# Two-layer hybrid backbone on one core: gate and up products of the feed-forward blocks recast as seven quarter products, with the way down in six groups

## The chip, the cores and the metric

The kernel runs on one core of a Trainium2 chip. The metric is the device time of one execution in microseconds (us). All arithmetic is float32. A large matrix product is made of three passes: each operand is split into a rounded part ("hi", the type that TensorE takes in one pass, fp32r in the rows) and the rest ("lo"), and hi*hi, hi*lo and lo*hi are added up in PSUM.

## The reference, cut to what matters

There are 512 latent tokens and 256 context tokens, width 1024, and two layers. Each layer has a first feed-forward block, a mixer (input projection, four kinds of heads, output projection), and a second feed-forward block:

```
h  += 0.5 * gate1 * (silu(m @ Wg) * (m @ Wu)) @ Wdown      m = rmsnorm(h) * gain * (1 + scale) + shift
u   = modulated rmsnorm(h) @ W_in ; h += gate2 * heads(u) @ W_out
h  += 0.5 * gate3 * (silu(m @ Wg) * (m @ Wu)) @ Wdown
```

Wg and Wu are 1024 x 2816, Wdown is 2816 x 1024. Shift, scale and gate come from a conditioning product ("mod") that the kernel works out in the shadow of other work. So there are four feed-forward blocks. Three of them have all 768 tokens (called wide below); in the last one context tokens are no longer needed, so that it has 512 (called narrow).

## The kernel before, in words

Activations lie transposed: 128 features on the partitions, tokens along the free axis. The residual `h` is 8 tiles of 128 x 768. A weight block is 128 output columns by 1024 rows, 512 KB, as 8 tiles of 128 x 128.

The function `ffn` (from L539) is one feed-forward block. It goes over 22 pairs of blocks (one of gate, one of up), in two halves of 11, and after each half takes that half's 11 results through the way down: 8 output tiles, each the sum over 11 blocks of 128. For each weight block SyncE (SP) loads `raw[s]` (L207), ScalarE rounds it to `w_hi[s]` (`split_hi`, L217), VectorE makes `w_lo[s] = raw - w_hi` (`split_lo`, L222), and TensorE runs `product` (L240). Gate uses slot 0 and up slot 1, so that while TensorE works on one slot the other one is refilled:

```python
for k in range(kt):
    for w, m in ((w_hi[s], mov_hi), (w_hi[s], mov_lo), (w_lo[s], mov_hi)):
        for a, b, o in spans:
            mm = pe.matmul(out[:, o:o + b - a], w[:, k, :], m[:, k, a:b], ...)
```

With 768 tokens and two shift columns, `spans` are 512 and 258 columns; with 512 tokens they are 258 and 258. So a pair is 96 matmuls: 2 blocks x 8 k x 3 passes x 2 spans. The moving operand `hn_hi`/`hn_lo` is h times gain, without the norm's 1/rms; that factor (`rstd`) is multiplied in when a product leaves PSUM (L647 for gate, L657 for up). For this reason the first product of a block can begin before the sum of squares is known: `sums_pe` (L479) runs behind the first gate product, and ScalarE makes `rstd` by Ln (L467) and Exp (L471) after that. After a gate product ScalarE does Tanh and Identity (L600, L602), VectorE the silu product (L652) and the gated product (L663), and `g_hi`/`g_lo` are made by ScalarE (L607) and VectorE (L668).

On the way down `add_residual` (L533) adds a finished tile to `h` from PSUM, ScalarE and VectorE make the next phase's `hn_hi` (L447) and `hn_lo` (L457) from it, and GpSimd (POOL) adds its square up (`square_residual`: L500, L503, L505). GpSimd has nothing else to do in a feed-forward block. The three wide blocks also work out 24 columns of mod each: VectorE takes two products of 128 x 1024 for each (L287).

The queues are in order: SP issues the loads in the order of use, each behind a wait for the buffer; each engine runs its list. Loops are hardware loops except at the edges. Each phase is a `Block`, at whose start all engines begin together.

Of the kernel before, what the change touches and what calls it, by code (L numbers as in the profile page):

```python
# [14 lines left out]
F32 = mybir.dt.float32  # L15
# [57 lines left out]
def build_trunk(nc, A):  # L73
    with ExitStack() as ctx:
# [35 lines left out]
        WS = NFH * P * 4  # L110
# [18 lines left out]
        gate, glu = out_sb  # L129
        tanh_g = tmp("tanh_g", [P, NT])  # L130
# [54 lines left out]
        gate_scaled, up_scaled = sem("gate_scaled", 1), sem("up_scaled", 1)  # L185
# [138 lines left out]
        def setup():  # L324
            n_setup = [0]
            with nc.Block() as block:
# [12 lines left out]
                def _(pool):  # L339
                    for x in lo_ready + block_done + evacuated + shifted + [gate_scaled, up_scaled] + mod_used:  # L340
                        pool.sem_inc(x.sem, 1)
# [196 lines left out]

        def ffn(l, which, nt, following, mod_plan=None, more=True, fresh=False, nxt=None):  # L539
            part = 0 if which == 0 else 6  # L540
            gain = "n1" if which == 0 else "n2"

            PER_HALF = NFH + KD // 2

            MODS = (NFH + 2, NFH)
            ml, mj0 = mod_plan or (0, 0)
            mod_from = (mj0, mj0 + MODS[0])

            with nc.Block() as block:
                @block.sync  # L550
                def _(sp):
                    for half in range(2):
                        b0 = half * PER_HALF
                        j0 = mod_from[half]
                        def step(i, loads=True):
                            for s in range(2 if loads else 0):
                                load_block(sp, s, A["wgu"][l, which, i * 2 + (half * NF + s)], KD, i + b0)
                            if mod_plan:
                                mod_load(sp, ml, 0, i + j0, i + half * MODS[0])
                        if half == 0:  # L560
                            step(0, loads=False)
                        with sp.Fori(1 if half == 0 else 0, NFH) as i:
                            step(i)

                        def load_down(i):
                            for s in range(2):
                                load_block(sp, s, A["wdn"][l, which, half, i * 2 + s], NFH, i + (b0 + NFH))
                        load_down(0)
                        if mod_plan and half == 0:
                            for n in range(NFH, MODS[0]):  # L570
                                mod_load(sp, ml, 0, j0 + n, n)
                        with sp.Fori(1, KD // 2) as i:
                            load_down(i)
                    next_loads(sp, following, KD, 2 * PER_HALF)

                @block.gpsimd
                def _(pool):
                    if more:
                        square_residuals(pool, KD // 2)

                @block.scalar
                def _(act):
                    act.preload_act_table_set("natural_log_exp_and_others")
                    if fresh:
                        split_hi(act, 0, KD, 0)
                        shifts_hi(act, l, part, nt)
                        for k in range(KD - 1):
                            gained_hi(act, k, nt)
                    gained_hi(act, KD - 1, nt)
                    split_hi(act, 1, KD, 0)  # L590
                    rstd_act(act, nt, True)

                    def gate_up(i, half, last):
                        b0 = half * PER_HALF
                        nk = NFH if last else KD

                        split_hi(act, 0, nk, i + (b0 + 1))
                        act.wait_ge(gate_scaled.sem, i + gate_scaled.at(half * NFH + 1))
                        for span, w in tokens_of(nt):
                            act.activation(tanh_g[:, span], gate[:, span], ACT.Tanh, bias=gate[:, nt + w:nt + w + 1])  # L600
                        for span, w in tokens_of(nt):
                            mm = act.activation(gate[:, span], gate[:, span], ACT.Identity,  # L602
                                                bias=gate[:, nt + w:nt + w + 1])
                        mm.then_inc(tanh_ready.sem, 1)
                        split_hi(act, 1, nk, i + (b0 + 1))
                        act.wait_ge(glu_ready.sem, i + glu_ready.at(half * NFH + 1))
                        act.activation(g_hi[:, bass.ds(i, 1), 0:nt].rearrange("p a t -> p (a t)"), glu[:, 0:nt],  # L607
                                       ACT.Copy).then_inc(g_hi_ready.sem, 1)

                    def down(i, half, last):  # L610
                        for s in range(2):
                            if not last:
                                split_hi(act, s, NFH, i + (half * PER_HALF + NFH + 1))
                            elif half == 0:
                                split_hi(act, s, KD, PER_HALF)
                            elif s == 0 and following:
                                split_hi(act, 0, KD, 2 * PER_HALF)
                            if half == 1 and nxt and not (last and s == 1):
                                gained_hi_after(act, s, i * 2 + s, nxt[3], i + evacuated[s].at(KD // 2 + 1), nxt[4])
                    for half in range(2):  # L620
                        with act.Fori(0, NFH - 1) as i:
                            gate_up(i, half, False)
                        gate_up(NFH - 1, half, True)
                        if half == 1 and nxt:
                            shifts_hi(act, nxt[0], nxt[2], nxt[3], 1, nxt[4])
                        with act.Fori(0, KD // 2 - 1) as i:
                            down(i, half, False)
                        down(KD // 2 - 1, half, True)

                @block.vector  # L630
                def _(dve):
                    if fresh:
                        norm_gains(dve, l, gain, part)
                        shifts_lo(dve, l, part, nt)
                        split_lo(dve, 0, KD, 0)
                        for k in range(KD - 1):
                            gained_lo(dve, k, nt, hn_hi_ready.at(k + 2))
                    sums_dve(dve, nt, True)
                    gained_lo(dve, KD - 1, nt, hn_hi_ready.at(KD + 1))
                    split_lo(dve, 1, KD, 0)  # L640
                    dve.wait_ge(rstd_ready.sem, rstd_ready.at(1))

                    def gate_up(i, half, last):
                        b0 = half * PER_HALF
                        nk = NFH if last else KD
# [55 lines left out]
                def _(pe):  # L701
                    def gate_up(i, half, first=False, is_first=False):
# [6 lines left out]
                        if first:  # L709
                            sums_pe(pe, nt)  # L710
# [1897 lines left out]
```

## Time and profile before

| | |
|---|---|
| median of 3 runs | 3361.91 us (3359.94 to 3364.61) |
| profiled execution | 3367.02 us, span 3365.3 us |
| mean granted TensorE clock | 0.985 |
| PE busy | 3231.2 us, 96% of the span |
| VectorE (DVE) busy | 1817.0 us, 54% |
| ScalarE (ACT) busy | 1157.8 us, 34% |
| GpSimd (POOL) busy | 439.7 us, 13% |
| DMA | 263.34 MB, mean 78 GB/s |

PE is TensorE's matmuls and PEld its weight loads, which run beside them. "A x2" in a row of a timeline is two instructions merged; a duration of one matmul is longer than its distance to the next one, since they are pipelined, so that rates are read from how many there are in a stretch. Of the four feed-forward blocks the wide ones take from 46 to 610, 1278 to 1839 and 1841 to 2402 us of the span, the narrow one 2978 to 3356.

### The profile page before, as it was taken

What the parts mean: (1) busy time and instruction counts of PE and PEld (TensorE: products, weight loads), DVE (VectorE), ACT (ScalarE), POOL (GpSimd) and SP (SyncE); (2) the same over time, 40 slices, a digit from 0 to 9 for tenths busy, and PEclk for the clock granted to TensorE, in tenths of its full rate; (3) what the DMA queues carried; (4) which work ended last, traced back from release to release, by engine and by line L of the source; (5) the groups of instructions that cost most, each with busy time, mean ns of one, the idle gap of its engine ahead of it and who ended that gap; (6) DMA issues with size and microseconds to landing.
All of it is one profiled execution on the core that took longest, in us unless ns stands there. A gap on an engine that the chain in (4) does not pass through costs nothing. (4 is left out here: it accounts for less than half of the span.)

```text
span 3365.3 us, 67083 instructions
## 1 busy us (share of the span) xinstructions
PE 3231.2 (96%) x28066; PEld 2765.1 (82%) x28066; DVE 1817.0 (54%) x2677; ACT 1157.8 (34%) x1839; POOL 439.7 (13%) x312
## 2 busy tenths in 40 slices
PE   6999999999988999999999999999999989899998
PEld 5888888886667878888888888888886668789897
DVE  4552554565667655543554553454555766655353
ACT  3331222225665333321222431222224654344231
POOL 2000001000705310000002000001100616120000
PEclk9999999999999999999999999999999999999999
DMA  5231221342000012222221222222232000122222
GB/s 201 91 109 66 94 96 60 127 156 89 1 17 3 4 57 81 93 98 77 90 90 57 94 98 71 81 93 85 85 141 110 2 18 3 34 88 94 90 91 94
DMA packets 68270, 263.34 MB, mean 78 GB/s; under 512 B 7552, under 2 KB 8704, under 8 KB 67456
## 3 DMA queue, kind: packets, MB, share of 16 engines
q1 hardware_dynamic: 67664, 256.95, 22.1%
q10 hardware_dynamic: 432, 3.88, 0.3%
q8 instruction: 133, 2.18, 0.3%
q14 instruction: 41, 0.34, 0.0%
HBM read 258.70 MB, written 2.10 MB: 77 GB/s over the span
## 5 line engine op out<-in xcount | busy, mean ns | idle before, releaser
L240 PE MATMUL ps<-hn_hi,w_hi 128*128 128x512 f32 (+1 forms) x3520 | 864.8, 327 | 17.9 <-DVE hn_lo L457 5.9
L240 PE MATMUL ps<-hn_hi,w_lo 128*128 128x512 f32 (+1 forms) x3520 | 865.4, 327 | 0.0
L240 PE MATMUL ps<-hn_lo,w_hi 128*128 128x512 f32 (+1 forms) x3520 | 861.1, 326 | 0.0
L217 ACT ACTIVATE w_hi<-raw 128x1024 fp32r<-128x1024 f32 (+1 forms) x300 | 338.5, 1128 | 1375.4 <-PE ps L240 1217.7
L222 DVE TENSOR_TENSOR w_lo<-raw,w_hi 128x1024 fp32r<-128x1024 f32 (+1 forms) x300 | 396.9, 1323 | 469.5 <-ACT w_hi L217 462.0
L240 PEld LDWEIGHTS ps<-hn_hi,w_hi 128*128 128x128 f32 x3520 | 547.9, 190 | 82.3 <-issue 17.6
L240 PEld LDWEIGHTS ps<-hn_lo,w_hi 128*128 128x128 f32 x3520 | 548.3, 190 | 58.3
L240 PEld LDWEIGHTS ps<-hn_hi,w_lo 128*128 128x128 f32 x3520 | 545.2, 190 | 58.1
L240 PE MATMUL ps<-g_hi,w_hi 128*128 128x512 f32 (+1 forms) x1424 | 398.0, 347 | 6.1 <-DVE g_lo L894 6.1
L240 PE MATMUL ps<-g_lo,w_hi 128*128 128x512 f32 (+1 forms) x1424 | 403.5, 351 | 0.0
L240 PE MATMUL ps<-g_hi,w_lo 128*128 128x512 f32 (+1 forms) x1424 | 397.5, 347 | 0.0
L240 PEld LDWEIGHTS ps<-g_hi,w_lo 128*128 128x128 f32 x1424 | 228.5, 189 | 39.6
L240 PEld LDWEIGHTS ps<-g_hi,w_hi 128*128 128x128 f32 x1424 | 224.7, 188 | 43.7 <-DVE w_lo L222 6.9
L240 PEld LDWEIGHTS ps<-g_lo,w_hi 128*128 128x128 f32 x1424 | 226.7, 189 | 34.5
L500 POOL TENSOR_TENSOR out_sb<-h 128x768 f32<-128x768 f32 x5 | 7.3, 1469 | 1602.0 <-DVE h L533 1602.0
L647 DVE TENSOR_TENSOR out_sb<-ps,rstd 128x770 f32<-128x770 f32 (+1 forms) x88 | 78.6, 894 | 242.6 <-PE ps L240 215.7
L657 DVE TENSOR_TENSOR out_sb<-ps,rstd 128x770 f32<-128x770 f32 (+1 forms) x88 | 78.6, 894 | 183.7 <-PE ps L240 183.7
L607 ACT ACTIVATE g_hi<-out_sb 128x768 f32 (+3 forms) x88 | 69.9, 795 | 211.1 <-DVE out_sb L663 211.1
L668 DVE TENSOR_TENSOR g_lo<-out_sb,g_hi 128x768 f32 (+3 forms) x88 | 78.5, 892 | 93.4 <-ACT g_hi L607 93.4
L287 DVE SCALAR_TENSOR_TENSOR ps<-w_mod_one,cond_rows 128x1024 f32<-128x1024 f32 x100 | 122.8, 1228 | 10.7 <-DMA w_mod_one<-wmod 9.7
L287 DVE SCALAR_TENSOR_TENSOR w_mod_one<-w_mod_one,cond_rows 128x1024 f32<-128x1024 f32 x100 | 122.1, 1221 | 0.0
L457 DVE SCALAR_TENSOR_TENSOR hn_lo<-h,moda,hn_hi (+1 forms) x88 | 92.6, 1095 | 51.4 <-ACT hn_hi L447 51.3
(274 smaller groups left out, 3795.8 us busy)
## 6 DMA issues: line engine op xcount, KB each, us to landing
raw<-wgu SPq DMA_DIRECT2D x176, 512.0 KB, 3.4
w_mod_one<-wmod SPq DMA_DIRECT2D x100, 512.0 KB, 3.3
raw<-wdn SPq DMA_DIRECT2D x64, 704.0 KB, 4.1
raw<-win SPq DMA_DIRECT2D x44, 512.0 KB, 4.5
w_mod_two<-wmod SPq DMA_DIRECT2D x28, 512.0 KB, 3.6
w_mod_first<-wmod_first SPq DMA_DIRECT2D x4, 2048.0 KB, 23.2
raw<-wout SPq DMA_DIRECT2D x16, 512.0 KB, 3.3
h<-xT ACTq DMA_DIRECT2D x1, 3072.0 KB, 9.8
```

What stands on the lines that cost most here:

```text
L217: act.activation(w_hi[s][:, 0:kt, :].rearrange("p k n -> p (k n)"), raw[s][:, 0:kt * P], ACT.Copy).then_inc(hi_ready[s].sem, 1)
L222: dve.tensor_tensor(w_lo[s][:, 0:kt, :].rearrange("p k n -> p (k n)"), raw[s][:, 0:kt * P], w_hi[s][:, 0:kt, :].rearrange("p k n -> p (k n ...
L240: mm = pe.matmul(out[:, o:o + b - a], w[:, k, :], m[:, k, a:b], start=(k == 0 and w is w_hi[s] and m is mov_hi), stop=(k == kt - 1 and w i ...
L287: mm = dve.scalar_tensor_tensor(out=products if w else ps[:, 4:7:2, :], in0=products, scalar=1.0, in1=cond_rows[:, w, :].rearrange("p (a b ...
L457: mm = dve.scalar_tensor_tensor(out=hn_lo[:, bass.ds(tile, 1), to].rearrange("p a t -> p (a t)"), in0=h[:, bass.ds(tile, 1), span].rearran ...
L500: pool.tensor_tensor(sum_sq[:, 0:NT], hv, hv, ALU.mult).then_inc(sq_summed.sem, 1)
L607: act.activation(g_hi[:, bass.ds(i, 1), 0:nt].rearrange("p a t -> p (a t)"), glu[:, 0:nt], ACT.Copy).then_inc(g_hi_ready.sem, 1)
L647: dve.tensor_tensor(slot_like(gate, nt), slot_all(0, nt), slot_like(rstd, nt), ALU.mult).then_inc(gate_scaled.sem, 1)
L657: dve.tensor_tensor(slot_like(glu, nt), slot_all(1, nt), slot_like(rstd, nt), ALU.mult).then_inc(up_scaled.sem, 1)
L668: dve.tensor_tensor(g_lo[:, bass.ds(i, 1), 0:nt].rearrange("p a t -> p (a t)"), glu[:, 0:nt], g_hi[:, bass.ds(i, 1), 0:nt].rearrange("p a ...
```

## The change

In `ffn`, the gate block and the up block side by side are a matrix of 2 x 2 quarters: gate and up across, the first and the second 512 rows down. The moving operand is cut likewise: first and second 512 features, first and second half of the tokens. Before, their product is eight quarter products. The change forms them from seven, by the known scheme (Strassen's, in Winograd's form), with sums and differences of quarters on both sides.

- **TensorE**: a pair is 7 products x 4 k x 3 passes = 84 matmuls of 386 columns (258 in the narrow block), each product into one PSUM bank, eight banks in turn. The code is unrolled and has no hardware loops.
- **The moving side** is made once for each feed-forward block, at its start. `x_norm` is h times gain times `rstd` (so `rstd` has to be known before the first matmul), then come T1 to T4, differences and sums of its quarters, and hi and lo of all seven. VectorE, GpSimd and ScalarE share this. The sum of squares is moved in front of it all, with the last tile's squares on ScalarE.
- **The weight side** is made for every pair: four sums or differences of quarters (128 x 512), on GpSimd (on VectorE for the first pair), each written into the lo slot of its product as soon as that product of the pair before is done; then hi of the gate block (128 x 1024) and of five quarters by ScalarE, and lo of the gate block and of two quarters by VectorE, of three by GpSimd.
- **Out of PSUM**: ScalarE copies the first product, VectorE does seven additions of one bank each, and Tanh, silu, the gated product and the split are done in two halves of the tokens.
- **The way down** is in six groups of 4, 2, 4, 4, 4 and 4 pairs in place of two of 11. Of the first four output tiles all blocks but the group's last are taken first, then the last one of each; tiles 4 to 7 follow whole. `h` is added to 8 times in each group. While a group's down products run, the next pair's weights are made.
- Mod columns are still 24 in each wide block, 11 of them beside gate and up work and 13 on the way down. In `out_proj` (L864) and at the end of a feed-forward block that another follows, only the gained h is written (`gained_plain`), and the `hn_lo` work of VectorE goes. The host lays `wdn` out anew, with the same bytes.

The core of the diff:

```diff
-        WS = NFH * P * 4
+        WS = KD * P * 4 + 1568
...
+        SIZES = DOWN_SIZES
...
+            def weight_sum(eng, p, n):
+
+                a, b, op = {2: (quarter(2), quarter(3), ALU.add),
+                            3: (slot_sum[2][:, :], quarter(0), ALU.subtract),
+                            4: (quarter(0), quarter(2), ALU.subtract),
+                            5: (quarter(1), slot_sum[3][:, :], ALU.subtract)}[p]
+                if n:
+                    slot_free(eng, p, n)
...
+                eng.tensor_tensor(slot_sum[p][:, :], a, b, op).then_inc(w_summed.sem, 1)
...
+                    def up_raw_free(n):
+                        sp.wait_ge(w_summed.sem, w_summed.at(4 * n + 4))
+                        lo_there(sp, 6, n)
...
+                    pool.wait_ge(hn_hi_ready.sem, hn_hi_ready.at(KD + 1))
+                    for half in range(2):
+                        pool.wait_ge(rstd_ready.sem, rstd_ready.at(half + 1))
+                        pool.tensor_tensor(x_norm[:, half, LP:KD, 0:HT], gained_h[:, LP:KD, half * HT:(half + 1) * HT],
+                                           rstd_of(half), ALU.mult).then_inc(x_pool.sem, 1)
+                        moving_lo((1, 5)[half], lambda k: x_norm[:, half, LP + k.start:LP + k.stop, 0:HW], (5, 11)[half])
+                    slot_lo_made(pool, 4, 0)
+                    slot_lo_made(pool, 3, 0)
+                    moving_lo(3, lambda k: m_raw[3][:, k, 0:HW], 13, "T4b")
+                    slot_lo_made(pool, 6, 0)
+
+                    def next_pair(n, first):
+
+                        for p in (2, 3, 5) if first else (2, 3, 4, 5):
+                            weight_sum(pool, p, n)
+                        slot_lo_made(pool, 3, n)
+                        slot_lo_made(pool, 6, n)
+                        if first:
+                            weight_sum(pool, 4, n)
+                        slot_lo_made(pool, 4, n)
...
+                            gate_first(n)
...
+                            with_sixth(n)
+                            with_fifth(n)
+                            if not last_of(n):
+                                slot_lo_made(dve, 2, n + 1)
...
+                            with_seventh(n)
+                            for m in mods_of.get(n, ()):
+                                mod_product(m)
+                            gate_second(n)
+                            up_first(n)
+                            silu(n, 0)
+                            glu_out(n, 0)
+                            silu(n, 1)
+                            glu_out(n, 1)
+                            if not last_of(n):
+                                slot_lo_made(dve, 5, n + 1)
+                            ring_lo_made(n, 0)
+                            ring_lo_made(n, 1)
...
+                                for w, m in ((slot_hi[p], M_OF[p][0]), (slot_hi[p], M_OF[p][1]), (slot_lo[p], M_OF[p][0])):
+                                    mm = pe.matmul(bank(n, p), w[:, k, :], m[:, k, 0:HW],
...
+                        together = 4
+                        for t in range(together):
+                            down(j, t, range(z - 1))
+                        for t in range(together):
+                            down(j, t, (z - 1,))
+                        for t in range(together, KD):
+                            down(j, t, range(z))
...
+DOWN_SIZES = (4, 2, 4, 4, 4, 4)
```

## Rows read from the trace of the kernel before

**Rows 1.** Page, part 1: busy time of each engine over the span.
```profile
PE 3231.2 (96%) x28066; PEld 2765.1 (82%) x28066; DVE 1817.0 (54%) x2677; ACT 1157.8 (34%) x1839; POOL 439.7 (13%) x312
```

**Rows 2.** Chain that ended last, in order of time: start us, us, what.
```profile
2987.45 369.12 PE ps L240 x2592
3356.57 0.03 issue
3356.59 0.75 DVE h L533
```

**Rows 3.** Stretches of matmuls alone (L240): PE busy, PEld busy, clock, DMA share, GB/s.
```profile
516.43:609.66 93.23, 93.23 (x530) 80.83 (x528) 1.00 0.15 50
621.06:799.35 178.29, 178.29 (x1008) 155.82 (x1008) 1.00 0.41 145
1559.09:1745.59 186.50, 186.50 (x1058) 163.17 (x1057) 1.00 0.28 93
3109.08:3168.85 59.77, 59.77 (x266) 49.50 (x265) 1.00 0.28 93
3168.93:3296.48 127.55, 127.55 (x1057) 127.54 (x1056) 1.00 0.28 92
```

**Rows 4.** Timeline at the start of a wide block: PE, then ACT.
```profile
1277.90 0.59 PE L240 MATMUL ps<-hn_hi,w_hi 128*128 128x512 f32 x2 [1.76 <-PEq L859]
...
1286.46 1.46 PE L479 MATMUL ps<-out_sb,const 128*128 128x384 f32 x4
1287.45 0.81 PE L240 MATMUL ps<-hn_hi,w_hi 128*128 128x512 f32 x2
...
1277.61 1.28 ACT L583 ACT_TABLE_LOAD   x1 [5.15 <-PEq L859]
1278.91 1.12 ACT L447 ACTIVATE hn_hi<-h,moda 128x512 fp32r<-128x512 f32 x2
...
1287.95 0.90 ACT L467 ACTIVATE lnv<-ps,small 128x768 f32<-128x768 f32 x1 [6.97 <-PE ps L479]
1288.88 0.94 ACT L471 ACTIVATE rstd<-lnv,small 128x768 f32<-128x768 f32 x1
```

**Rows 5.** Timeline at the start of the narrow block, PE.
```profile
2977.99 0.77 PE L240 MATMUL ps<-hn_hi,w_hi 128*128 128x258 f32 x2 [3.31 <-PEq L859]
...
2980.70 0.63 PE L240 MATMUL ps<-hn_hi,w_hi 128*128 128x258 f32 x2
2981.13 0.63 PE L240 MATMUL ps<-hn_lo,w_hi 128*128 128x258 f32 x2
```

**Rows 6.** Instruction groups by shape, DVE, whole span: busy us, mean ns, idle before.
```profile
L222 DVE TENSOR_TENSOR w_lo<-raw,w_hi 128x1024 fp32r<-128x1024 f32 x236 | 292.9, 1241 | 175.6 <-ACT w_hi L217 168.1
L647 DVE TENSOR_TENSOR out_sb<-ps,rstd 128x770 f32<-128x770 f32 x66 | 63.3, 960 | 209.5 <-PE ps L240 189.8 <-ACT rstd L471 19.7
L657 DVE TENSOR_TENSOR out_sb<-ps,rstd 128x516 f32<-128x516 f32 x22 | 15.3, 696 | 57.1 <-PE ps L240 57.1
L2261 DVE TENSOR_TENSOR x_inv<-masks,ps 128x256 f32<-128x256 f32 x24 | 10.0, 418 | 10.3 <-PE ps L2025 10.3
L287 DVE SCALAR_TENSOR_TENSOR ps<-w_mod_one,cond_rows 128x1024 f32<-128x1024 f32 x100 | 122.8, 1228 | 10.7 <-DMA w_mod_one<-wmod 9.7
```

**Rows 7.** The same view, POOL.
```profile
L1742 POOL TENSOR_TENSOR ar<-ar,u 128x768 f32<-128x768 f32 x3 | 5.5, 1824 | 0.2
L1742 POOL TENSOR_TENSOR ar<-ar,u 128x512 f32<-128x512 f32 x3 | 3.8, 1276 | 0.2
L1529 POOL TENSOR_TENSOR shift_prev<-u,cols 128x512 f32<-128x512 f32 x3 | 3.1, 1041 | 7.7 <-DVE keep L1549 7.6
```

**Rows 8.** Timeline, POOL and DVE side by side, both reading SBUF alone.
```profile
2969.71 2.18 POOL L505 TENSOR_TENSOR out_sb<-out_sb,h_sq 128x768 f32<-128x768 f32 x1
...
2969.04 1.14 DVE L457 SCALAR_TENSOR_TENSOR hn_lo<-h,moda,hn_hi  x1 [1.15 <-ACT hn_hi L447]
2970.43 2.54 DVE L222 TENSOR_TENSOR w_lo<-raw,w_hi 128x1024 fp32r<-128x1024 f32 x1 [0.25 <-ACT w_hi L217]
```

**Rows 9.** Timeline, POOL and DVE side by side, DVE reading PSUM.
```profile
2785.56 1.81 POOL L1745 TENSOR_TENSOR bk<-bk,f 128x768 f32<-128x768 f32 x1
...
2786.47 0.96 DVE L2284 COPY b_nat<-ps 128x768 f32<-128x768 f32 x1 [1.58 <-PE ps L1995]
```

**Rows 10.** DMA issues of the narrow block: KB each, median us to landing.
```profile
raw<-wgu SPq DMA_DIRECT2D x40, 512.0 KB, 3.2
```

**Rows 11.** All engines over one wide and the narrow block (PE, PEld, DVE, ACT, POOL).
```profile
1277.00:1838.00 561.00, 560.10 (x3167) 488.26 (x3168) 280.18 (x345) 157.85 (x200) 23.50 (x13) 1.00 0.25 84
2977.00:3356.00 379.00, 378.01 (x2643) 357.40 (x2644) 166.39 (x188) 124.76 (x139) 0.39 (x1) 0.99 0.27 89
```

More of the change, by code:

```diff
@@ new lines, in x_block, with halves, inner @@
+            def x_block(half, k0, k1):
+                return x_norm[:, half, k0:k1, 0:HW]
+            def halves(half):
+                a = half * HT
+                return [(slice(max(span.start, a) - a, min(span.stop, a + HT) - a), w) for span, w in tokens_of(nt)
+                        if min(span.stop, a + HT) > max(span.start, a)]
+            C = (slice(0, HT), slice(HW, HW + HT))
+            shift_of = lambda x, w: x[:, HT + w:HT + w + 1]
+            def inner(half, s):
+                return slice(C[half].start + s.start, C[half].start + s.stop)
@@ L551, in _ @@
                 def _(sp):
[L552 to L573, printed above, removed]
@@ L593, in gate_up @@
[L593 to L608, printed above, removed]
@@ L610, in down @@
[L610 to L619, printed above, removed]
@@ L620, in _ @@
-                    for half in range(2):
[L621 to L628, printed above, removed]
+                            gained_plain(act, k, nt)
@@ new lines, in _ @@
+                    for i in range(2):
+                        t = slice(i * HT, (i + 1) * HT)
+                        act.activation(h_sq[:, t], h[:, KD - 1, t], ACT.Square).then_inc(sum_ready.sem, 1)
+                    act.wait_ge(moda_ready.sem, moda_ready.at(2))
+                    gained_plain(act, KD - 1, nt)
+                    for half in range(2):
+                        mm = act.activation(x_norm[:, half, :, HT:HW], shifts_of(l, part), ACT.Copy, scale=0.5)
+                    mm.then_inc(hn_hi_ready.sem, 1)
@@ L672, in down @@
-                    def down(i, half, last):
-                        done = half * PER_HALF + NFH
-                        for s in range(2):
-                            if not last:
-                                split_lo(dve, s, NFH, i + (done + 1))
-                            elif half == 0:
-                                split_lo(dve, s, KD, PER_HALF)
-                            elif s == 0 and following:
-                                split_lo(dve, 0, KD, 2 * PER_HALF)
-                            add_residual(dve, s, i * 2 + s, nt, part + 2, i + block_done[s].at(done + 1))
-                            if half == 1 and nxt and not (last and s == 1):
-                                gained_lo(dve, i * 2 + s, nxt[3], i * 2 + hn_hi_ready.at(KD + 1 + s + 2), nxt[4])
@@ L684, in _ @@
[L684 to L693 removed]
+                        whole_lo(1)
@@ L2461, in layout @@
     A["wgu"] = np.stack(gus, 1)
[L2462 removed]
+    A["wdn"] = np.stack([down_loads(w) for w in (ffn1_w_down, ffn2_w_down)], 1)
     z64 = np.zeros((L, D_MODEL, 64), f)
```

696 lines of the change are left out of this document (590 added, 106 removed).

## The prediction

> **What bounds the kernel now.** The page's first part has PE at 96% of the span, with VectorE at 54 and GpSimd at 13 [rows 1]; the chain that ended last is one piece of 369 us of matmuls [rows 2]. Over a whole feed-forward block PE is busy 560 of 561 us, and 378 of 379 in the narrow one [rows 11]. So fewer columns are worth time at once, unless the engines around TensorE fall behind: VectorE is busy half of such a block, and GpSimd 24 and 0.4 us of it.
>
> **1. Matmuls taken away.** The wide pairs run at 186.50 / 11 = 16.96 us, the narrow ones at 127.55 / 11 = 11.60 us, 0.1208 us for a matmul of 258 columns; the 264 matmuls of 512 in a narrow way down take 59.77 us, 0.2264 each [rows 3]. Between the two, 386 columns cost 0.1208 + 128/254 x 0.1056 = 0.174 us. The wide pair's mixed spans give 0.1766 for 385 as the upper end. 84 x 0.174 = 14.62 us for a wide pair, 2.33 less; 84 x 0.1208 = 10.15 for a narrow one, 1.45 less. 66 x 2.33 + 22 x 1.45 = 154 + 32 = **186 us off** (172 at the upper end). The way down keeps its matmuls (93.23 us for 11 pairs [rows 3]) and the loads their bytes. Of the unrolled code I take no cost: the input projection is unrolled too, and its 1008 matmuls take 178.29 us, 0.177 each [rows 3].
>
> **2. The start of a feed-forward block.** Before, the first matmul comes 0.3 us after the block's start and `rstd` is made beside it: the first wide pair is through at 1287.45 + 8.5 = 1295.9, 18.3 us after the start [rows 4]; in the narrow block PE begins at half clock (0.43 us for two matmuls of 258, against 0.24), and its second product ends near 2992.9, 15.2 us after the start [rows 5]. Afterwards nothing can begin before `rstd`: table load 1.3, two squares 1.1, last tile's gain 1.1, shifts and a weight half 1.0, Ln and Exp by halves 1.5, together 6.1 us by the durations of [rows 4] (5.6 narrow).
>
> Then the moving side. Its size is set by how VectorE and GpSimd go together. GpSimd's addition of 768 takes 1.82 alone [rows 7], 2.18 where it began behind a VectorE instruction with two SBUF inputs, and VectorE's `w_lo`, 1.23 alone, took 2.54 beside it: it stood still for 1.31 of the 1.46 us of overlap [rows 8]. Beside GpSimd, VectorE's copy from PSUM keeps its 0.96 [rows 9]. So the two take turns as soon as VectorE reads SBUF twice, with about 0.15 us given back at one hand-over and 0.1 at the other. The Trainium skill, "SBUF — State Buffer", section "Who interferes with whom", says it as a rule: the pair of ports is an exclusive lock for a whole instruction, and the later one blocks fully. The trace agrees, but for those 0.25 us; by the bare rule each turn below would cost 0.17 more, some 2 us a block.
>
> All of this work reads SBUF twice. VectorE, by [rows 6] (0.42 for 256, 0.70 for 516, 0.96 for 770, 1.24 for 1024; 0.08 less each, back to back): 14 instructions of 772 at 0.88, 8 of 386 at 0.48, two weight halves at 0.61, one of 1536 at 1.7: 19.0 us. GpSimd, by [rows 7] (2.1 ns a column and 0.18, less 0.17 a turn): two of 1536 at 3.27, six of 772 at 1.65, three weight halves at 1.10: 19.7 us. In turns 38.7 us, all before the seventh product. GpSimd writing fp32r is in no row; I take it like f32 (between 1.04 and 1.28 for 512, nearest the latter, whose operands are two tiles). The first pair ends at 6.1 + 38.7 + 2.1 = 46.9, and 1.6 more since PE is idle or sparse for so long that some of it is at half clock as in [rows 5]: 48.5 us. Narrow: 5.6 + 13.8 + 14.3 + 1.5, and 0.8: 36 us. The cost on top of part 1 is 48.5 - 18.3 + 2.3 = 32.5 wide, three times, and 36 - 15.2 + 1.45 = 22.3: **120 us on**. Bounds: 28 and 37 wide, 19 and 26 narrow, by other ways in which the turns fall.
>
> **3. The narrow block's steady state.** For each next pair in a group GpSimd has seven additions or subtractions of 512: four sums, lo of products 3, 6 and 4. The up block's load waits for lo of product 6 (its last reader), takes 3.2 us [rows 10], and then come the four sums, lo 3 and lo 6 again. That circle is 3.3 + 6 x 1.27 = 10.9 us, already over the 10.15 of PE. In it VectorE cuts in with what reads SBUF twice: two weight halves, two silu and two gated products of 256, 2.7 us in all, of which I take 1.6 (the rest falls into the time of the load). So 12.5 us, 2.4 late, in the 16 passes from pair to pair within a group: **38 us on**. Low end: additions as short as the row of 1.04 [rows 7], 9.5 us, no delay. High end: all VectorE's port work of a pair, 4.6 us, cut in: 15.5, 86 us. I take the middle, since most additions of two tiles are at 1.27.
>
> **4. The wide blocks' steady state.** The same circle with 386 columns is 12.7 to 15 us against 14.62: mostly hidden. Two places stick out: the first group, where GpSimd comes from the start-up with no lead (the up block's load begins at 45 us, and lo of product 4 is some 3 us late), and the 11 pairs with a mod column, whose 2.45 us [rows 6] also read SBUF twice: port work 7.7 on GpSimd and 5.4 + 2.4 on VectorE, 15.5 us against 14.62, most of it taken by the lead from the way down. I take 5 us a block, **15 us on** (0 to 45). ScalarE has some 8 us of work a pair and is hidden.
>
> **5. The way down.** Six groups bring 32 more residual additions a block, 1.14 us each from PSUM, spread over 186 us of matmuls: nothing. Between a group's last product and its `g_lo` lie about 5 us on VectorE and ScalarE (up addition, two silu, two gated, two splits). The order "four tiles' other blocks first" covers that with 36 matmul pairs, 12.7 us, in groups of four (8.1 narrow) but only with 12 pairs, 4.2 (2.7 narrow), in the group of two: a stall of 1 to 2 us once a block, within part 4. SP waits in order, but what it waits for comes in that order.
>
> **Sum.** -186 + 120 + 38 + 15 = -13 us. The profiled execution has 3367.0, 5.1 over the median; so 3354 for it and 3349 for the median. About 0.2% (6.7 us) is what a measurement of this kernel can tell from no change.
>
> **Rivals.** *A, as summed* (own range 3325 to 3380): a large gain, most of it given back. Chance 0.45: over 0.2% faster 0.29, the same 0.08, slower 0.08.
>
> *B, GpSimd's circle sets the narrow block, and slower than before.* If VectorE cuts in with nearly all its port work, the circle is 14.5 to 15.5 us; it costs 70 to 86 us in place of 38, also at the groups' starts, where lo of product 4 waits behind tile 7. The narrow block is then longer than its 379 us and the whole 3349 + 45 = 3394. It decides from 13 us a circle (3357) on. For it: GpSimd's order is rigid, and the load is inside the circle. Against: VectorE's instructions may fall into the 3.3 us of the load. Chance 0.30: slower 0.27, same 0.03.
>
> *C, the turns cost little.* GpSimd at 1.04 and VectorE in its gaps: no term 3, a start of 28 wide: 3349 - 38 + 4 = about 3310. For it: busy time alone fits everywhere (wide pair VectorE 10.2 us, GpSimd 8.9, PE 14.6). Against: [rows 8]. Chance 0.20, all faster.
>
> *D, the change doesn't save what it says:* if 386 columns cost like 512 (0.2264), a wide pair takes 19.0 us and the kernel gets over 100 us longer. Against: [rows 3] scale with the columns. Chance 0.05, slower.
>
> **How the numbers follow.** Faster 0.29 + 0.20 = 0.49, the same 0.11, slower 0.40. The range goes from most of C to beyond B's middle: 3303 to 3410.
>
> **What would show it.** Matmuls of 386 about 0.174 us apart; the first matmul of a wide block some 10 us after its start and its first pair done at 48; VectorE instructions of two SBUF inputs far over their own length beside GpSimd, and those with PSUM input not; in the narrow block PE waiting for lo of products 3 or 4 by GpSimd, pairs at 12.5 us within a group against 10.15; the narrow block about as long as before (379) or longer, the wide ones about 15 us shorter (561). Wrong would be a first pair done by 30 us, or no growth of those VectorE instructions; then the sum falls towards C.

## The result and the profile after

The changed kernel takes **3559.8 us** (median of 4, 3557.7 to 3567.0), the kernel before beside it 3363.3 (3359.9 to 3365.0): ratio 1.059, interval 1.057 to 1.061. It is 197 us slower; the forecast was 3349, and the range ended at 3410. The busy times of the profile of after, to be read against [rows 1]:

```profile
PE 3161.1 (89%) x27026; PEld 2790.4 (78%) x27026; DVE 2454.4 (69%) x3739; ACT 1408.6 (40%) x2643; POOL 1543.9 (43%) x1028
```

From one stretch's last matmul to the next one's:

| us | before | after | difference |
|---|---|---|---|
| first block (wide) | 569.5 | 612.2 | +42.7 |
| second block of layer 1 (wide) | 562.9 | 588.5 | +25.5 |
| first block of layer 2 (wide) | 563.0 | 604.0 | +41.0 |
| last block (narrow) | 381.9 | 448.8 | +66.9 |
| both mixers | | | +18.5 |

The third and the fourth as stretches of all engines (columns as in [rows 11]), and behind them the matmuls alone of four wide pairs late in the third:

```profile
1915.70:2519.70 604.00, 537.35 (x2912) 502.19 (x2912) 460.85 (x633) 220.87 (x401) 307.20 (x195) 0.95 0.23 79
3099.50:3548.30 448.80, 375.27 (x2385) 337.24 (x2384) 309.51 (x439) 185.96 (x341) 268.95 (x180) 0.97 0.22 76
...
2413.50:2472.90 59.40, 59.29 (x336) 59.29 (x336) 1.00 0.25 84
```

TensorE, busy throughout in [rows 11], is now idle for 67 of 604 us and 74 of 449. Where nothing stalls, the last row gives 59.3 / 4 = 14.83 us a wide pair, 0.1766 a matmul. The lengths of pairs (one's first matmul to the next one's, the last of a group to its own last matmul) show where it does stall. "D" is a way down, from its first matmul to its last one; what passes from there to the next pair's first matmul is in no entry. The first entry of a block is its first pair, from its first matmul on. A wide block (the second) and the narrow one:

```
wide    36.0 20.0 20.0 16.6 D38.0 | 14.9 15.0 D18.5 | 14.8 14.8 17.0 19.7 D35.0 | 16.5 16.5 19.6 16.6 D35.1
        14.9 14.8 14.8 15.0 D33.8 | 14.8 14.8 14.8 15.0 D33.8
narrow  26.4 18.2 13.6 13.5 D22.5 | 12.5 14.2 D15.8 | 10.1 14.4 14.7 12.2 D22.5 | 12.8 14.2 13.6 13.5 D22.5
        14.0 12.7 13.6 13.5 D22.5 | 14.0 12.6 13.6 13.5 D22.5
```

Wide pairs are at full pace in the last two groups and slow in groups 0, 2 and 3, the ones with mod columns (pairs 1 to 3 and 6 to 13; 6 and 7 still keep pace). Narrow pairs are slow nearly everywhere. The ways down of groups 0, 2 and 3, which have mod columns too, last 35.0 to 38.0 us and not 33.8, and behind each another 1.9 to 2.3 us pass in this block until the next pair begins, since its first bank waits for VectorE's additions to `h`, which stand behind the mod products:

```profile
1471.43 0.41 PE L1260 MATMUL ps<-m_hi,w_hi 128*128 128x386 f32 x1 [1.85 <-DVE h L1113]
```

The two blocks that a mixer follows end with a way down of 46.3 and 46.7 us in place of 33.8, and 5.1 to 5.4 us (1.65 before) until the mixer begins. The first mixer starts 3.8 and the second 3.4 us later by that; most of the other 11 us of the last line of the table are in the heads, whose code is the same. Between the first block's last matmul and the second block's first one the changed kernel takes 689 us, e1 682 and e5 691, so those 11 us are not shown to come from the change.

**The start**, as VectorE and GpSimd in the second block, which begins at 1327.2:

```profile
1334.21 4.25 DVE L1127 TENSOR_TENSOR x_norm<-gained_h,rstd_s 128x384 f32<-128x384 f32 x2 [2.78 <-ACT rstd_s L949]
...
1334.26 3.79 POOL L826 TENSOR_TENSOR x_norm<-gained_h,rstd_s 128x1536 f32<-128x1536 f32 x1 [8.51 <-ACT rstd_s L949]
1342.24 5.45 POOL L821 TENSOR_TENSOR m_lo<-x_norm,m_hi 128x772 fp32r<-128x772 f32 x2 [4.19 <-ACT m_hi L926]
```

VectorE's two instructions of 384 columns, 0.55 each elsewhere, take 4.25 beside GpSimd's one: turns, as predicted. The first pair is through at 1375.1, 47.9 us after the start (48.5 predicted). From its first matmul on the granted clock is 0.70 on average:

```profile
1339.00:1375.10 36.10, 23.20 (x84) 20.61 (x85) 33.46 (x26) 16.74 (x24) 23.62 (x10) 0.70 0.03 8
```

**The narrow circle**, a piece of the chain that ended last (start us, us, what). Here and below "sum 2" is the sum or difference written into the lo slot of product 2, "hi 6" and "lo 6" are the two parts of product 6's weights:

```profile
3414.64 1.53 POOL slot_lo L715
3416.26 3.31 DMA raw<-wgu
3419.62 0.09 issue
3419.71 1.31 POOL slot_sum L706
3421.09 0.09 issue
3421.18 2.25 POOL slot_sum L706
3423.80 1.35 issue
3425.15 0.47 DVE up_s L1067 x2
3425.62 0.19 issue
3425.81 0.42 DVE gate_s L1067
3426.26 0.18 ACT tanh_s L911
3426.43 0.24 issue
3426.67 0.49 ACT gate_s L913
3427.17 0.52 ACT pair_hi L877
3427.68 0.53 ACT slot_hi L877
3428.28 1.51 POOL slot_lo L715
```

From one lo 6 to the next: 13.64 us, and no TensorE in it. The load comes in (3419.57), then sums 2 and 3; sum 3, 1.29 alone, takes 2.25 beside VectorE's `w_lo`; only then can VectorE make lo 2 (1.70 us long, since it stands beside sum 4: the "issue" of 1.35), and behind that lo in its list are the additions for which ScalarE's second tanh waits; behind the tanh in ScalarE's list stands hi 6, for which GpSimd's lo 6 waits, and the next load for that.

### The profile page after: what moved, and what is told of

Its sections match the earlier page's. It is cut to its first block and busy times, and to the rows that moved or that the text cites. A ratio compares the mean times of both kernels' runs of the same rounds, so it can differ in the third digit from the quotient of the medians.

```text
span 3557.0 us, 66836 instructions
## 1 busy us (share of the span) xinstructions
PE 3161.1 (89%) x27026; PEld 2790.4 (78%) x27026; DVE 2454.4 (69%) x3739; ACT 1408.6 (40%) x2643; POOL 1543.9 (43%) x1028
## 5 line engine op out<-in xcount | busy, mean ns | idle before, releaser
L1260 PE MATMUL ps<-m_hi,pair_hi 128*128 128x386 f32 (+1 forms) x1408 | 480.8, 342 | 147.6 <-POOL slot_lo L715 106.2
L1260 PE MATMUL ps<-m_lo,pair_hi 128*128 128x386 f32 (+1 forms) x1408 | 470.8, 334 | 0.0
L1260 PEld LDWEIGHTS ps<-m_hi,pair_hi 128*128 128x128 f32 x1408 | 278.0, 197 | 170.2 <-POOL slot_lo L715 119.8
L1260 PE MATMUL ps<-m_hi,slot_lo 128*128 128x386 f32 (+1 forms) x1056 | 352.8, 334 | 0.0
L1260 PE MATMUL ps<-m_hi,w_hi 128*128 128x386 f32 (+1 forms) x704 | 237.8, 338 | 57.9 <-DVE m_lo L1046 24.2
L1260 PEld LDWEIGHTS ps<-m_lo,pair_hi 128*128 128x128 f32 x1408 | 278.8, 198 | 0.0
L1260 PE MATMUL ps<-m_hi,w_lo 128*128 128x386 f32 (+1 forms) x704 | 235.3, 334 | 0.0
L1260 PE MATMUL ps<-m_lo,w_hi 128*128 128x386 f32 (+1 forms) x704 | 235.1, 334 | 0.0
L1260 PE MATMUL ps<-m_hi,pair_lo 128*128 128x386 f32 (+1 forms) x704 | 232.8, 331 | 0.0
L238 PE MATMUL ps<-hn_hi,w_hi 128*128 128x512 f32 (+1 forms) x704 | 175.5, 331 | 12.1 <-PEq L763 10.5
```

What stands on the lines that cost most here:

```text
L1260: mm = pe.matmul(bank(n, p), w[:, k, :], m[:, k, 0:HW], start=(k == 0 and w is slot_hi[p] and m is M_OF[p][0]), stop=(k == LP - 1 and w is ...
```

## The experiments

Differences are to the changed kernel, by the two ratios to the kernel before on the same chips (0.01 is 33.6 us). The interval of each ratio is about 6 us either way, so that of a difference is about 9. e3, e5, e6, e12 and e14 leave work out and have another output; they are there to be measured. The letters of the theories are those of the expectations: P, turns at the ports and GpSimd's durations; L, the order of VectorE's list; C, the circle through the load; S, the sum of both engines' time at the ports; M, the size of the mod product; V, VectorE's time a tile.

### The pairs: list, ports, load

**e1** moves `slot_lo_made(dve, 2, n + 1)` down:

```diff
-  slot_lo_made(dve, 2, n + 1)
   with_seventh(n)
   ...
   gate_second(n)
+  slot_lo_made(dve, 2, n + 1)
```

> VectorE's lo of the next pair's product 2 goes behind the addition of product 5 (three places later in VectorE's list), nothing else moves. In the changed kernel that lo waits for GpSimd's sum 3, which waits for the up block's load, and ScalarE's second tanh, lo 6 and with it the next load wait behind it. Theory L (order of VectorE's list closes the circle): a narrow pair within a group falls from 13.4 us to about 12.6 (3.4 of load and six GpSimd instructions of 1.3, with one or two turns), wide pairs 1 to 3 of a block from 20 to under 17, and the whole gets 25 to 60 us shorter. Theory P (the turns at the SBUF ports and GpSimd's own durations set the circle): the narrow pair stays over 13.0, the whole gains less than 10 us.

3532.2 us, ratio 1.049: **-32 us**. But narrow pairs (mean of all from the third on) went only from 13.4 to 13.0, and that block is only 4 us shorter; pairs 1 to 3 of a wide block are at 21.0, 16.4, 18.8. The order has a part in it and is not the cause by itself.

**e3** narrows VectorE's lo of the gate block:

```diff
-  dve.tensor_tensor(whole(pair_lo[0]), raw[0][:, 0:KD * P], ...)
+  dve.tensor_tensor(whole(pair_lo[0])[:, 0:32], raw[0][:, 0:32], ...)
```

> VectorE's lo of the gate block (1024 columns, two SBUF inputs, 1.2 us alone and 1.6 us here on average) takes 32 columns in every pair but a block's first, so most of it is left out and the output is another one. GpSimd's sum 3 stood 0.94 us beside it in each stalled narrow pair. Theory P: the narrow pair loses 0.9 to 1.3 us (13.4 to about 12.3), wide pairs with mods about 1 us each, 25 to 45 us in all. Theory L: GpSimd is freed but the list still holds the second tanh behind the load, the load's end moves by the same turn only: under 0.5 us a pair, under 15 us in all.

3527.3 us, 1.048: **-37 us**, narrow block 434.8 (-14). As theory P has it in the whole; per narrow pair 0.6, less than the 0.9 to 1.3 that it said.

**e5** narrows GpSimd's work of the pairs:

```diff
-  eng.tensor_tensor(slot_sum[p][:, :], a, b, op)
+  eng.tensor_tensor(slot_sum[p][:, c], a[:, c], b[:, c], op)      # c: 32 columns on GpSimd from pair 1 on, also in slot_lo
```

> GpSimd's seven sums and los of every pair but a block's first take 32 columns in place of 512 (most of that work is left out; ScalarE and VectorE keep their sizes but read a stand-in, so the output is another one); every wait, load and order stays, and so do the los of the way down. Theory P (GpSimd's durations and turns carry the circle): the narrow pair falls from 13.4 us to 10.2, wide pairs with mods to about 15, 70 us off the narrow block and 15 to 30 off each wide one, 110 to 150 in all. Rival, the list and the load carry it by themselves: narrow pairs stay over 11.5 us and the whole gains less than 60.

3391.8 us, 1.006: **-178 us**, more than expected. Its busy times:

```profile
PE 3120.1 (92%) x27026; PEld 2769.4 (82%) x27026; DVE 2207.9 (65%) x3739; ACT 1405.4 (41%) x2643; POOL 869.3 (26%) x1028
```

VectorE's busy time falls by 246 us without one of its instructions being made narrower: that is what it stood beside GpSimd's work in the pairs. All narrow pairs from the third on are at 10.1 and the narrow block takes 376.0 us; wide pairs from the third on are at 14.8, those with mods too (the first of a group at 14.9, once at 16.5), and wide blocks are 31 to 33 us shorter. So nine tenths of the loss hang on GpSimd's work in the pairs; the lists, waits and loads, all still there, stall next to nothing in the pairs without it. The ways down with mods stay at 35 us and more, with 1.3 to 2.0 behind them. This also rules out two other causes: the unrolled code, since the same code keeps pace here, and the clock, since the mean granted clock is 0.963 here and 0.960 in the changed kernel.

**e10** is e1 with two of GpSimd's instructions on VectorE:

```diff
 def next_pair(n, first):
-  slot_lo_made(pool, 3, n)
+  if first: slot_lo_made(pool, 3, n)
   slot_lo_made(pool, 6, n)
   ...
   up_first(n)
+  slot_lo_made(dve, 3, n + 1)
   silu ... glu_out(n, 1)
+  slot_lo_made(dve, 4, n + 1)
```

> On top of the reordered list: lo of products 3 and 4 of a next pair within a group goes from GpSimd to VectorE; nothing is left out. By theory P what counts is the ports' time of both engines together: 1.28 us twice on GpSimd become 0.61 twice on VectorE, and the circle through the load loses two GpSimd instructions: narrow pairs from 13.2 us (the reordered list) to about 11.8, wide pairs with mods to about 16, 30 to 45 us faster than the reordered list alone (3532). Rival: VectorE's in-order list, 1.2 us longer, is the next limit: less than 10 us.

3513.3 us, 1.042: **-57 us**, 25 better than e1: just short of the range. Pairs 8 to 13 of the second block fell from 17.6 to 15.9 on average, narrow pairs only to 13.0, where they were in e1, though 2.6 us of GpSimd were gone from their circle.

**e12** halves the up block's load within a group:

```diff
-  load(1, A["wgu"][l, which, 2 * n + 3])
+  sp.dma_start(raw[1][:, 0:LP * P], A["wgu"][l, which, 2 * n + 3][:, 0:LP * P])
```

> The up block's load inside a group brings 512 of its 1024 columns (the second half keeps older data, so the output is another one); nothing else changes. Theory C (a circle: load, four sums, lo 3, lo 6, next load): the load falls from 3.4 us to about 2, each narrow pair within a group loses 1.2 to 1.5 us (13.5 to 12.2), wide pairs with mods about 1, 35 to 55 us in all. Theory S (the ports' time of both engines in sum: GpSimd 7 x 1.28 and VectorE 4.6 make 13.6 in a narrow pair, and 16.8 in a wide one with a mod): nothing changes, under 8 us in all.

3539.8 us, 1.052: **-24 us**. Half the bytes were not half the time (KB each, median us to landing):

```profile
raw<-wgu SPq DMA_DIRECT2D x112, 512.0 KB, 3.3
raw<-wgu SPq DMA_DIRECT2D x64, 256.0 KB, 2.7
```

0.6 us less of load, and the later narrow pairs of a group went from 13.6 and 13.5 to 12.9 and 12.3, 0.6 to 1.2 less. Port work had not changed, so theory S (the sum of the ports' time sets the narrow pair; under 8 us in all) falls there, close as its 13.6 was: it is a circle with the load in it. The whole stays short of theory C's 35 to 55 us, which reckoned with a load of 2 us.

### The mod columns

**e6** makes the mod products that stand in pairs 32 columns wide:

```diff
+  c = slice(0, 32 if n in (0, 1, 2, 8, 9, 10, 11, 16, 17, 18, 19) else D_MODEL)
   dve.scalar_tensor_tensor(out=w_mod[0][:, c] ..., in0=w_mod[0][:, c], in1=cond_rows[:, w, c], ...)
```

> The 11 mod products of a wide block that stand in gate and up pairs (pairs 1 to 3, 8 to 13) take 32 columns in place of 1024, so most of that work is left out and the output is another one; those in the way down stay. Theory M (a mod product's 2.45 us at the SBUF ports, ahead of the addition that the second tanh waits for, is what stalls the wide pairs): pairs 8 to 13 fall from 16.5 to 19.7 us to 14.8, pairs 1 to 3 from 20, 20 and 16.5 to at most 17, 24 to 33 us off each wide block, 75 to 100 in all; the narrow block, which has none, stays at 449. Rival C (the circle through the load stalls the first group by itself, mods or none): pairs 1 to 3 stay near 19, and the whole gains 30 to 55.

3494.1 us, 1.037: **-73 us**, just short of theory M's 75 to 100, none of it in the narrow block (451.5). Pairs 6 to 13 are at 14.8 to 15.0 but for the first of a group, pairs 1 to 3 at 20.1, 16.5 and 15.0: theory M, but for pair 1. That pair 1 inherits the start's delay is not shown by this run; without GpSimd's work (e5) it takes 15.3.

**e7** puts the columns into the ways down of groups 0 to 4 (`mods_of["down", j]` = 5, 5, 5, 5, 4; in the first block pairs 1 to 3 keep theirs).

> Nothing is left out: the mod columns of the wide blocks go into the ways down of groups 0 to 4 (five, five, five, five, four; in the first block pairs 1 to 3 keep theirs and groups 1 to 4 take four each). Theory M: pairs as without mods, 14.8 us, but each way down with mods costs about 1.2 us more and the pair behind it 1.6 (as 35.0 against 33.8 and 16.5 against 14.8 show), so 10 to 20 us off a wide block and 35 to 60 in all. Rival: the way down of the group of two (18 us) can't hold five loads and products, the next pair's loads stand behind them on SP, and the stall only moves: under 20 us in all.

3552.8 us, 1.054: **-15 us**, the rival. The pairs of the second and third block are at full pace but for pair 1 and the first of a group, but the group of two's way down takes 32.0 and 33.8 us there in place of 18.5, with 4.0 and 1.9 behind it.

**e13** moves a pair's product behind its last split:

```diff
-  for m in mods_of.get(n, ()): mod_product(m)
   gate_second(n)
   ...
   ring_lo_made(n, 1)
+  for m in mods_of.get(n, ()): mod_product(m)
```

> The mod product of a pair stands behind the pair's last split on VectorE and not ahead of the addition of product 5; nothing is left out. Theory L (its place delays the second tanh, lo 6 and the next load by 2.45 us): wide pairs 8 to 13 fall from 17.6 us on average to 15.5 or less, pairs 1 to 3 by 1 to 2 each, 45 to 65 us in all. Theory S (9.0 + 5.4 + 2.45 = 16.8 us of port work a pair): they stay at 16.8 or more, under 20 us in all.

3678.9 us, 1.092: **113 us slower**, which neither theory had. SP's queue in that run:

```profile
2227.45 0.33 SPq L277 DMA_DIRECT2D w_mod_one<-wmod  x1
2227.87 0.86 SPq L772 DMA_DIRECT2D raw<-wgu  x2
2249.83 0.33 SPq L277 DMA_DIRECT2D w_mod_one<-wmod  x1
```

The mod's load waits for the last product to leave the buffer (VectorE ends it at 2227.41), and both blocks of the next pair stand behind it on SP. Pairs take up to 23.7 us.

**e16** takes that queue out: the same, and `load_mods(n)` behind the pair's two loads.

> The mod product of a pair behind the pair's last split, as in the run before, and its load behind the pair's two block loads on SP and not ahead of them; nothing is left out. Theory L (place in VectorE's list): wide pairs 8 to 13 at 15.5 us or less, 45 to 65 us faster than the changed kernel. Theory S (port work of both engines, 16.8 us a pair with a mod): these pairs at 16.8 us on average against 17.6, 10 to 20 us faster in all. In both, the 113 us that the late product alone had cost are gone.

3563.5 us, 1.057: -5 us, no difference, less than either theory said. The 113 us are gone. Pairs 8 to 13 of the second block take 17.2, 15.5, 14.9, 17.5, 17.9 and 15.5, on average 16.4 (17.6 in the changed kernel), between the two theories and nearer to S (9.0 of GpSimd, 5.4 and 2.45 of VectorE at the ports are 16.8, against 14.83 of TensorE); and what the pairs gain the ways down lose, 38.1 for 35.0. Another place for the product brings nothing; without its size (e6) 73 us go.

### The ways down

**e4** undoes the order of the way down: `together = 4` becomes `together = 0`.

> Only the order of TensorE's way down is undone: each tile takes its whole group at once, as before the change, in place of four tiles' other blocks ahead. If that order does what it is for, 4 to 7 us come back as a stall at each of the 24 groups' ways down (up addition, two silu, two gated products and two splits behind the last product): 80 to 150 us slower. Rival, the order is what makes the last way down late: with the first tile out some 12 us earlier VectorE starts its additions and gains of the mixer sooner, and the two last ways down ahead of the mixer come back from 46 to about 40 us each; that alone would be 12 us faster, so the whole would be 70 to 140 slower in place of it.

3645.5 us, 1.084: **84 us slower**. Ways down take 37 to 44 us wide, some 30 narrow (22.5). The order is worth this much here. It is not the cause of the late mixer: the last ways down went from 46.3 to 42.0, but the mixer began 7.2 us behind them in place of 5.4.

**e8** makes tile 7's hi and lo after the third tile (`t == 2` for `t == 5`, both engines). What it is about, in the changed kernel (TensorE, then VectorE):

```profile
2502.00 0.51 PE L1284 MATMUL ps<-ring_hi,slot_lo 128*128 128x512 f32 x2
2513.15 1.01 PE L1284 MATMUL ps<-ring_hi,pair_hi 128*128 128x512 f32 x2 [10.65 <-DVE slot_lo L735]
...
2508.39 3.05 DVE L455 SCALAR_TENSOR_TENSOR hn_lo<-h,moda,hn_hi 128x512 fp32r<-128x512 f32 x2 [1.19 <-ACT hn_hi L445]
2511.37 1.13 DVE L1113 SCALAR_TENSOR_TENSOR h<-ps,mod,h 128x512 f32<-128x512 f32 x2
2512.42 0.68 DVE L735 TENSOR_TENSOR slot_lo<-raw,pair_hi 128x512 fp32r<-128x512 f32 x1
```

> In a block's last way down, tile 7's hi and lo are made when the third tile has been added and not after the sixth; nothing else moves. The last ways down ahead of the mixer take 46.3 and 46.7 us against 33.8, and TensorE stands 10.7 us before tile 7. Theory S (that wait is on the path): 10 to 12 us come back twice, 20 to 24 us off the whole. Rival V: VectorE's additions and gains for the mixer, 5.3 us a tile beside GpSimd's squares and without a gap from 7 us after the first tile on, end the stretch themselves: TensorE's wait only moves behind tile 7, and the whole gains under 4 us.

3567.9 us, 1.058: **no difference**, rival V. The wait went elsewhere, from tile 7 to the mixer's first matmul:

```profile
638.52 0.51 PE L1286 MATMUL ps<-ring_hi,slot_lo 128*128 128x512 f32 x2
656.62 0.98 PE L238 MATMUL ps<-hn_hi,w_hi 128*128 128x512 f32 x2 [17.59 <-PEq L763]
```

**e14** is e8 with the squares small:

```diff
-  square_residuals(pool, LAST * KD // 2)
+  ... the same per tile, from tile 2 on with c = slice(0, 32)
```

> Tile 7's hi and lo early as in the run before, and GpSimd's squares and their additions in a block's last way down take 32 columns from the third tile on (most is left out, so the output is another one). Theory V (VectorE's 5.3 us a tile against TensorE's 4.2 set the stretch; 1.6 of these are its second gain standing beside GpSimd's addition): VectorE needs 3.7, the way down takes 33.8 us and the mixer's first matmul follows within 3 us in place of some 19, so 12 to 16 us come back twice, 24 to 32 in all. Rival (ScalarE's gains or the following loads set it): under 10 us.

3536.6 us, 1.051: **-27 us**, theory V in the whole. VectorE goes through a tile in 3.4 us (5.3 in the changed kernel), the way down takes 33.8, and the wait ahead of the mixer is 7.3 us and not 17.6 (nor the 3 expected):

```profile
644.03 0.98 PE L238 MATMUL ps<-hn_hi,w_hi 128*128 128x512 f32 x2 [7.34 <-PEq L763]
```

### The start, and the parts together

**e9** gives GpSimd's start-up work to VectorE: the two `x_norm` of 1536, six `m_lo` of 772 and three weight quarters, each ahead of the product that needs it.

> All of GpSimd's work at a block's start (x_norm of the second halves of the columns, lo of moving blocks 1, 5 and 3, lo of weight quarters 4, 3 and 6) goes to VectorE, in the order in which TensorE takes the products; nothing is left out. Theory P (the two engines take turns at the SBUF ports, so that a start lasts as long as their port work one after the other, 38.7 us by the prediction, and GpSimd needs about twice VectorE's time for the same columns): on VectorE alone it is some 19 + 10.5 us, so the first wide pair ends 8 to 10 us earlier (47.9 to about 39) and the narrow one 5 to 7, 30 to 36 us off the whole. Rival (they do work side by side): VectorE's list grows by 10 us, and the first pair ends later, 20 to 40 us on the whole.

3534.6 us, 1.049: **-34 us**. VectorE at the same place as above:

```profile
1324.10 1.03 DVE L1108 TENSOR_TENSOR x_norm<-gained_h,rstd_s 128x384 f32<-128x384 f32 x2 [2.79 <-ACT rstd_s L930]
...
1331.02 1.83 DVE L1125 TENSOR_TENSOR m_lo<-x_norm,m_hi 128x772 fp32r<-128x772 f32 x2 [0.31 <-ACT m_hi L907]
1336.39 1.75 DVE L1116 TENSOR_TENSOR x_norm<-gained_h,rstd_s 128x1536 f32<-128x1536 f32 x1
```

1.03 for 4.25, and what GpSimd did in 3.79 and 5.45 takes 1.75 and 1.83. The second pair begins at 41.4 us and not 47.9 (narrow 31.8 for 35.6). With 10 us more in its list, by its own durations, VectorE alone is done 6.5 us sooner than both engines were together. The four starts of the profiled execution are 24 us shorter in all; where the other 10 of the 34 are isn't shown.

**e11** joins e9, e10 and a better place for the mods (five each in the ways down of groups 0, 2, 3 and 4, four in pairs).

> The start on VectorE, the reordered list with lo of products 3 and 4 on VectorE, and the mod columns five to the way down of each group of four but the last, four in single pairs; nothing is left out. If the parts add up: 3560 less 33 for the start, 65 for list and los, and 40 to 55 for the mods, 3405 to 3425, still 40 to 60 us slower than the kernel before. Rival: the mods' place brings less once the ports are free, 3440 to 3460.

3458.6 us, 1.027: **-109 us**, the best version of the new scheme that was run, 90 us behind the kernel before; the rival's range. Wide blocks take 582, 558 and 577 us, the second 5 less than before the change; the narrow one 434.5.

**e15** is e11 with sum 5 on VectorE.

> The combined kernel, with sum 5 of a next pair within a group on VectorE too (behind the addition of product 5); GpSimd keeps three sums and lo 6. Nothing is left out. Both theories C and S let the narrow pair fall (by 1.28 in the circle, by 0.67 in the sum): from 12.9 us to 11.7 by C or 12.2 by S, the narrow block from 434 us to 414 by C or 424 by S; wide blocks change by under 3 us. Whole 3430 to 3445. Rival: VectorE, now at some 10 us a pair, is the limit, nothing gained.

3471.2 us, 1.032: 16 us slower than e11, the rival. The narrow block gains 2 us, the wide ones lose 4 to 7. In the narrow block's chain, between one lo 6 (3314.5) and the second after it (3341.8), 13 us now run through VectorE's list (3326.6 to 3339.8), but for 1.9 us of ScalarE within.

## Why the prediction was wrong

**1. Matmuls taken away: right**, at its upper end. 14.83 us a wide pair and 10.1 a narrow one without a stall, 172 us off in place of 186: 14 us of the error. The row of 385 columns at 0.1766 had said it; the interpolated 0.174 was too low.

**2. The start: right.** 47.9 and 35.7 us against 48.5 and 36, about 117 us on (120). The turns were sized rightly, and e9 shows that they and GpSimd's slower pace set it, not the length of VectorE's list. How much of it is the clock (0.70 in the first pair, for which the prediction took 1.6 us) no run tells apart.

**3. "12.5 us, 2.4 late, in the 16 passes": mis-sized, and short of a mechanism.** Measured are 13.9 on average in those 16 (18.2 in the first of them, 13.6 in the rest), and the first pairs of most later groups, which the 16 left out, are late too (12.5 to 14.0). By the table the term is 66.9 + 32 - 22 = 77 us, twice 38: 59 in the 16, 13 in the first pairs of groups, and 5 in the way down of the group of two (15.8 us for 48 matmuls, 10.9 at the 0.2264 of [rows 3]). This is rival B, given 0.30. I summed GpSimd's circle and asked only what cuts in at the ports. The chain shows that it also runs through two lists: hi 6 behind the second tanh on ScalarE, that tanh behind lo 2 on VectorE, lo 2 behind the load. e5, e12, e3 and e1 show GpSimd's work, the load, VectorE's port work and the order as parts of it. Why taking 2.6 us of GpSimd out (e10) gives back 0.3 a pair isn't settled; e15's chain says only that VectorE's list comes next.

**4. "I take 5 us a block": the step that failed most.** The three wide blocks grew by 109 us; 140 came off, 95 went on at the start, 25 belong to the last ways down, so this term is 129 us in place of 15. I had the sum, 15.5 us of work at the ports in a pair with a mod against 14.62, and called it "most of it taken by the lead from the way down". It was low, too: one of GpSimd's seven instructions takes about 1.3 us where nothing cuts in (1.30 and 1.29 at 3419.71 and 3423.39 in the narrow block), where I had reckoned 1.10, and with the turns their means are 1.42 to 1.60,

```profile
L706 POOL TENSOR_TENSOR slot_sum<-raw,slot_sum 128x512 f32<-128x512 f32 x84 | 134.3, 1598 | 21.9 <-PE ps L1284 10.5 <-PE ps L1260 9.2
...
L706 POOL TENSOR_TENSOR slot_sum<-slot_sum,raw 128x512 f32<-128x512 f32 x84 | 119.2, 1419 | 19.9 <-POOL slot_sum L706 11.5 <-PE ps L1260 7.4 <-PE ps L1284 1.0
```

and the lead was small: behind the group of two it carried pairs 6 and 7, behind the start and behind group 2 nothing. From there a pair hands its delay on whole. Of the 129 us some 91 are in the pairs behind a block's first; e6 leaves 30 of these and e5 8. The other 39 are in the ways down that have mods, and behind them, until the next pair begins: 13 a block, which neither this term nor "nothing" in part 5 had. e6 prices the mods in pairs at 73 us, e5 shows that they cost nothing once GpSimd's work is away, e16 that another place in the pair brings nothing. The range's 45 us for this term was two thirds too short, and this alone decides the case: with 129 for 15 the sum would have been 3463.

**5. The way down "nothing": wrong, most of all in two blocks.** "32 more residual additions a block ... spread over 186 us of matmuls" overlooked the last group (and the 39 us of part 4). Before, the last way down sums 11 blocks a tile, 11.7 us, and VectorE's 5.3 us a tile for the mixer (addition, two gains, one beside GpSimd's squares) hide in it. A group of four gives a tile 4.2 us. 25 us, and with it the 7 us by which the mixers start later: e8 and e14 show that it is VectorE's time a tile. The four tiles ahead did what the text said, and more (e4).

So of 205 us between sum and result (-13 against +192 in the profiled executions), about 114 are term 4, 39 term 3, 25 and 7 term 5 with the mixers' start, 11 the inside of the mixers (open), 14 the pace, and -3 the start; what is over is rounding and the two ends of the span.

## What to carry to other kernels

Work for idle engines is priced by what all of them share. GpSimd was only 43% busy, and its work in the pairs cost 178 us (e5): it and VectorE take turns, and it needs about twice the time a column (a sum of 512 columns takes 1.30 us there and 0.69 on VectorE, as in e9 at 1319.42). With this work on VectorE alone the start was 6.5 us shorter. Where a pair's port work exceeded TensorE's time, the lead covered two pairs here, and the rest was stall. Follow each wait through every in-order list until it closes (e13: a mod's load on SP held two weight blocks), and when work is cut into more groups, look at the last one, where the cover is shortest.

## What the runs showed of the hardware that I had not expected

A load of 256 KB landed after 2.7 us and one of 512 KB after 3.3 (e12). A short VectorE instruction can be made more than three times as long by its turn: a gated product of 256 columns, about 0.4 by [rows 6], took 1.40 where GpSimd had begun a lo of 512 columns 0.4 us before it, and ended 0.3 us behind that one (in the changed kernel, POOL and DVE):

```profile
3412.87 1.52 POOL L715 TENSOR_TENSOR pair_lo<-slot_sum,pair_hi 128x512 fp32r<-128x512 f32 x1
...
3413.28 1.40 DVE L1099 SCALAR_TENSOR_TENSOR up_s<-up_s,tanh_s 128x256 f32<-128x256 f32 x1
```
